# A two-block transformer kernel: expert queries and projection tiles as three one-pass products, and a table of zeros stored earlier

## The reference

```python
h = modulate(rmsnorm_2(x, norm1_g), shift1, scale1)
proj = h @ w_in                          # 1024 -> 512 + 128 + 128 + 3 * 512
q, k, v, cb, cc, cu = jnp.split(proj, SPLITS, axis=-1)
q = rope(rmsnorm_2(q, q_norm_g)); k = rope(rmsnorm_2(k, k_norm_g))
attn = sliding_window_attention(q, k, v, sinks)        # window 128, 8 heads, 2 kv heads
conv = cb * short_conv(cc * cu, conv_w)
merged = concatenate([rmsnorm_2(attn, attn_out_g), rmsnorm_2(conv, conv_out_g)])
x = x + gate1 * (merged @ w_out)
h2 = modulate(rmsnorm_2(x, norm2_g), shift2, scale2)
x = x + gate2 * peer(h2, wq, subkeys, u_tab, v_tab)
```

## Time and profile before

| | |
|---|---|
| time, median of 3 runs | 2406.66 us (2406.08 to 2408.51) |
| profiled execution, its own time | 2408.77 us |
| its span | 2407.0 us |
| mean granted TensorE clock | 0.992 |

### The profile page before, as it was taken

How to read it: one execution, slowest core, us unless ns; L and a number is a source line. 1 busy time by engine, 2 the same in 40 slices (tenths; PEclk the granted TensorE clock), 3 DMA queues, 4 the chain that set the end, 5 groups by cost and what they waited for, 6 DMA issues and landing times.

```text
span 2407.0 us, 33349 instructions
## 1 busy us (share of the span) xinstructions
PE 2371.8 (99%) x11315; PEld 1444.0 (60%) x11315; DVE 1445.1 (60%) x2831; ACT 874.4 (36%) x1385; POOL 1065.4 (44%) x739
## 2 busy tenths in 40 slices
PE   8999899999999999999999999999999999999999
PEld 6888677668888865445544444444444566666665
DVE  4512376366968456436948893222222498999998
ACT  3222134232232342223135555454545433333332
POOL 0001121010000020001888888888888165578886
PEclk9999799999999999999999999999999999999999
DMA  7240100165746313941446666666667799999997
GB/s 208 71 73 1 49 18 32 69 190 146 233 133 195 81 53 102 382 144 54 88 71 155 148 154 151 154 151 151 155 147 164 260 408 371 370 362 371 366 374 285
DMA packets 437699, 426.47 MB, mean 177 GB/s; under 512 B 104808, under 2 KB 359912, under 8 KB 437488
## 3 DMA queue, kind: packets, MB, share of 16 engines
q1 hardware_dynamic: 353456, 332.85, 43.3%
q0 software_dynamic: 84160, 92.58, 15.6%
HBM read 364.28 MB, written 61.05 MB: 177 GB/s over the span
## 4 chain that ended last, share of the span: by engine, by line
PE 86%; DVE 2%; ACT 1%; issue 0%; POOL 0%; DVEq 0%; ACTq 0%; POOLq 0%
PE psum L1473 9%; PE psum L1474 9%; PE psum L1475 9%; PE psum L1496 7%; PE psum L1498 7%; PE psum L1497 7%; PE psum L1248 6%; PE psum L1205 5%; PE psum L1207 5%; PE psum L1206 5%; PE psum L1454 4%; PE psum L968 1%; PE psum L1194 1%; PE psum L1092 1%; PE psum L988 1%; PE psum L1048 1%
## 5 line engine op out<-in xcount | busy, mean ns | idle before, releaser
L785 POOL DMA_INDIRECT dense_gates<-arena x384 | 607.2, 1581 | 151.6 <-issue 116.7
L1473 PE MATMUL psum<-arena 128*128 128x512 bf16 x1024 | 389.4, 380 | 0.0
L1475 PE MATMUL psum<-arena 128*128 128x512 bf16 x1024 | 387.2, 378 | 0.0
L1474 PE MATMUL psum<-arena 128*128 128x512 bf16 x1024 | 386.6, 378 | 0.0
L2542 DVE TENSOR_TENSOR arena<-arena,psum 128x1024 bf16<-128x1024 f32 x124 | 151.5, 1222 | 352.2 <-ACT psum L1854 351.6
L1497 PE MATMUL psum<-arena,low 128*128 128x384 bf16 x1024 | 333.8, 326 | 0.0
L1498 PE MATMUL psum<-arena,low 128*128 128x384 bf16 x1024 | 333.8, 326 | 0.0
L1496 PE MATMUL psum<-arena,low 128*128 128x384 bf16 x1024 | 333.8, 326 | 0.0
L1870 ACT ACTIVATE low<-low 128x1024 bf16<-128x1024 f32 x128 | 135.3, 1057 | 297.7 <-PE psum L1498 278.4
L813 POOL DMA_INDIRECT arena<-gelu_spill,arena x128 | 184.0, 1438 | 87.0 <-DMA gelu_spill<-cst 43.3
L805 POOL DMA_INDIRECT arena<-in_v,arena x128 | 177.4, 1386 | 86.7 <-DVE arena L2589 59.2
(11 more groups left out here) (378 smaller groups left out, 3910.5 us busy)
## 6 DMA issues: line engine op xcount, KB each, us to landing
arena<-in_uT SPq DMA_DIRECT2D x128, 512.0 KB, 4.6
low<-in_v SPq DMA_DIRECT2D x128, 512.0 KB, 5.5
gelu_spill<-cst SPq DMA_DIRECT2D x128, 256.0 KB, 3.4
arena<-in_ada_w POOLq DMA_DIRECT2D x12, 2048.0 KB, 9.3
dense_gates<-arena SPq DMA_DIRECT2D x4, 6144.0 KB, 40.0
arena<-gelu_spill SPq DMA_DIRECT2D x128, 192.0 KB, 5.7
arena<-dense_gates SPq DMA_DIRECT2D x128, 192.0 KB, 6.9
low<-in_w_in SPq DMA_DIRECT2D x20, 1024.0 KB, 7.3
```

The source lines that it names most:

```text
L785: pool.indirect_dma_start(gate_cells, bass.IndirectOffsetOnAxis(ap=cell_of[:, n:n + 1], axis=0), gate_of[:, n:n + 1], None, compute_op=ALU ...
L1473: mm(psum[:, bank, :], hi[:, c, :], h2hi[:, c, :], start=c == 0, stop=False)
L1474: mm(psum[:, bank, :], hi[:, c, :], h2lo[:, c, :], start=False, stop=False)
L1475: last = mm(psum[:, bank, :], lo[:, c, :], h2hi[:, c, :], start=False, stop=c == DC - 1)
```

## The change

Fifteen tiles of the second block's projection (n = 0, 1: the query tiles f = 2, 3; n = 2: the key tile; n = 3 to 14: the convolution) and the queries u = 2 to 15 are made from halves: ScalarE copies the weight tile into one of four float32r tiles (`s_high`, `q_high`), VectorE subtracts and writes the low half over the tile in its slot (`second_low`, `query_low`), and TensorE makes high x high and low x high over all chunks and then high x low. The modulated input is split too, chunk by chunk: on ScalarE the high halves; on GpSimd the low halves of chunks 0 to 4 (`LOWS_POOL`) in the second block and of all eight for the queries, on VectorE those of chunks 5 to 7 in the second block. The low half for the queries is written over `u2`, so GpSimd waits for the last half query too. `take_half` and `half_scores` move within ScalarE's order, `AHEAD` goes from 20 to 15 and `slots_of(1)` into `choose`. `zeros` lies in `turned`; GpSimd sets it before the first attention, and SP stores it in sixteen DMAs, two or three behind each load of gate sums; VectorE waits for them before its first use of `turned`.

```diff
-PARTS, AHEAD = 8, 20
+PARTS, AHEAD = 8, 15
+LOWS_POOL = 5
+ZEROS = 16
@@ SP, first attention, for h in range(FH)
                 sp.dma_start(cb[:, h % 2, :], sums[h:h + 1, :].to_broadcast([P, T])).then_inc(S[f"sums_in{h % 2}"], 16)
+                if h == 0:
+                    sp.wait_ge(S["pool_step"], 10)
+                else:
+                    for q in range((h - 1) * ZEROS // (FH - 1), h * ZEROS // (FH - 1)):
+                        sp.dma_start(io["dense"][q * PK // ZEROS:(q + 1) * PK // ZEROS, :, 0:DEN].rearrange("i j t -> j i t"),
+                                     zeros.unsqueeze(1).to_broadcast([P, PK // ZEROS, DEN])).then_inc(S["zeroed"], 16)
@@ SP, second block
-            sp.wait_ge(S["pool_step"], 10)
-            for q in range(4):
-                sp.dma_start(io["dense"][q * 32:(q + 1) * 32, :, 0:DEN].rearrange("i j t -> j i t"),
-                             zeros.unsqueeze(1).to_broadcast([P, 32, DEN])).then_inc(S["zeroed"], 16)
@@ GpSimd
+            for c in range(LOWS_POOL):
+                pool.wait_ge(*second_part("l2_sq", c + 1))
+                pool.tensor_tensor(s_operand_low[c], u2[:, c, :], s_operand_high[c], ALU.subtract).then_inc(S["g_nm"], 1)
...
+            for c in range(DC):
+                pool.wait_ge(S["h2_split"], c + 1)
+                pool.wait_ge(*operand_part("ffn_sil", c + 1))
+                pool.wait_ge(*operand_part("ffn_ps", c + 1))
+                pool.tensor_tensor(u2_low[c], u2[:, c, :], u2_high[c], ALU.subtract).then_inc(S["sq_sum"], 1)
@@ TensorE
+            def second_product(n, bank, sig, between=None):
+                pe.wait_ge(*second_part("x_nrm", n + 1))
+                wh, wl, out = s_high[n % 4], second_cols(n, slot_halves), psum[:, bank, :]
+                for c in range(DC):
+                    if n == 0:
+                        pe.wait_ge(*second_part("l2_sq", c + 1))
+                    if between and c == 4:
+                        between()
+                    mm(out, wh[:, c, :], s_operand_high[c], start=c == 0, stop=False)
+                    mm(out, wl[:, c, :], s_operand_high[c], start=False, stop=False)
+                for c in range(DC):
+                    if n == 0:
+                        pe.wait_ge(*(second_part("g_nm", c + 1) if c < LOWS_POOL else second_part("l2_done", c - LOWS_POOL + 1)))
+                    last = mm(out, wh[:, c, :], s_operand_low[c], start=False, stop=c == DC - 1)
...
@@ TensorE, expert queries
-                for c in range(DC):
-                    last = mm(psum[:, u % 2, :], w[:, c, cols], u2[:, c, :], start=c == 0, stop=c == DC - 1)
+                for c in range(DC):
+                    mm(out, wh[:, c, :], u2_high[c], start=c == 0, stop=False)
+                    mm(out, wl[:, c, :], u2_high[c], start=False, stop=False)
                     if u == 2 and c == 1:
                         for k in range(2):
                             half_scores(k, 1)
+                for c in range(DC):
+                    last = mm(out, wh[:, c, :], u2_low[c], start=False, stop=c == DC - 1)
@@ ScalarE, second block
-            shift(0, 0)
+            shift(0, 0, first_highs)
+            second_operand_high(0, 4)
...
+                if f == 0:
+                    second_operand_high(4, DC)
+                    second_high(2)
...
+                for n in {0: (7,), 1: (8,), 2: (9, 10), 3: (11,), 4: (12, 13), 5: (14,)}.get(s, ()):
+                    second_high(n)
@@ VectorE, second block
             modulated(0, col_n1, DC)
+            for n in range(2):
+                second_low(n)
+            for c in range(LOWS_POOL, DC):
+                dve.wait_ge(*second_part("l2_sq", c + 1))
+                dve.tensor_tensor(s_operand_low[c], u2[:, c, :], s_operand_high[c], ALU.subtract).then_inc(S["l2_done"], 1)
             dve.wait_ge(S["std_ready"], 5)
             settle(dve.reciprocal(r2[:, 1, :], r2[:, 1, :]))
...
                     last_norm(2 * j + 1)
+                if j == 0:
+                    second_low(2)
+            second_low(3)
+            second_low(4)
             rotate(4)
+            second_low(5)
...
+                for n in {0: (6,), 1: (7,), 2: (8,), 3: (9, 10), 4: (11,), 5: (12, 13), 6: (14,)}.get(s, ()):
+                    second_low(n)
@@ VectorE, choice of experts
+            lows = {(0, 2): 3, (0, 6): 4, (1, 4): 5, (1, 7): 6, (2, 2): 7, (2, 4): 8, (2, 7): 9}
+            for piece, (t0, t1) in enumerate(((0, 1), (1, 2), (2, SC))):
                 for part in range(PARTS):
+                    if (piece, part) in lows:
+                        query_low(lows[piece, part])
                     choose(0, part, t0, t1)
                 slots_of(0, t0, t1)
             for k in range(PARTS, AHEAD):
+                if k < PARTS + 6:
+                    query_low(k + 2)
                 choose(*divmod(k, PARTS))
```

More of the change, by code:

```diff
@@ L133, in program @@
         arena_floats = 53200 - n_const - 64
+        with nc.sbuf_tensor("split_low", [P, CUT], F32R) as split_low:
+            pass
         low = ctx.enter_context(nc.sbuf_tensor("low", [P, CUT], F32))
@@ L136, in program, with halves_room @@
             pass
+        def halves_room(name, at, n):
+            start = (at - CUT) // 8 * 8
+            lead = at - CUT - start
+            with ExitStack() as before:
+                if start:
+                    before.enter_context(nc.sbuf_tensor(f"before_{name}", [P, start], F32))
+                return before.enter_context(nc.sbuf_tensor(name, [P, lead + n], F32R))[:, lead:lead + n]
+        NORM_AT, LAST_AT, RING_AT = CUT, 28035, 35619
+        halves_norm = halves_room("halves_norm", NORM_AT, (DC + 2) * SEC)
+        halves_last = halves_room("halves_last", LAST_AT, 2 * SEC)
+        halves_ring = halves_room("halves_ring", RING_AT, 8665)
+        SECOND_AT = 36872
+        halves_second = halves_room("halves_second", SECOND_AT, 2 * DC * SEC + 4 * DC * P)
         arena = ctx.enter_context(nc.sbuf_tensor("arena", [P, arena_floats - CUT], F32))
@@ L710, in _ @@
             pool.memset(rstd[:, :, T:TP], 0.0).then_inc(S["pool_step"], 1)
+            pool.wait_ge(S["table_in"], 32)
+            step(pool.memset(zeros, 0.0))
             pool.wait_ge(S["gate_tok"], NT)
@@ L1416, in half_query @@
                               start=c == 0, stop=c == DC - 1)
-                if c == DC - 1:
+                    if half and u:
+                        last.then_inc(S["ffn_ps"], 1)
+                if c == DC - 1 and not (half and u):
                     last.then_inc(S["wq_done"], 1)
@@ L1780, in _ @@
                     qk_root(4)
+                    second_high(3)
+            for n in (4, 5, 6):
+                second_high(n)
             def take_c(j):
@@ L1835, in _, with query_high, take_half @@
             std2(5, 6, 0, eps)
+            def query_high(u):
+                if u in (2, 4, 8, 12):
+                    act.wait_ge(*fill_done(F_WQ + u // 4))
+                if u >= 6:
+                    act.wait_ge(S["wq_done"], u - 2)
+                f_(q_high[u % 4], q_raw(u), ACT.Copy).then_inc(S["fw_hi"], 1)
+            SH = SEC // 2
+            def take_half(u, half):
+                if half and u:
+                    act.wait_ge(*operand_part("ffn_ps", DC))
+                else:
+                    act.wait_ge(S["wq_done"], 2 * half + u + 1)
+                f_(qf[:, u, half * SH:(half + 1) * SH], psum[:, 6 * half + u, 0:SH], ACT.Copy).then_inc(S["wq_taken"], 1)
+            query_high(2)
             shift(1, 3 * DC)
@@ L1913, in _ @@
                 u_high(n + 3, n + 3, first=n == 0)
-                h = n // PARTS + 3
-                if n == 0:
-                    weigh_slots(2)
-                elif n % PARTS == PARTS - 1 and h < PH:
+                h, part = divmod(n + 1 + AHEAD, PARTS)
+                if part == 4 and h < PH:
                     weigh_slots(h)
```

149 lines of the change are left out of this document (107 added, 42 removed).

## The result

The changed kernel takes 2392.0 us in the median of five runs (2386.91 to 2393.64), the kernel before beside it 2406.66 (2405.11 to 2408.91): a ratio of 0.9932 with an interval from 0.9921 to 0.9944. It is faster, by 14.7 us or 0.7%, clear of the noise though a small gain, and my forecast of 2378.5 (2368 to 2390) was too low. The profiled execution took 2392.0 us with a span of 2390.2; the span of before was 2407.0, so the spans differ by 16.8 us where my sum had 27.9.

What follows compares the result with a forecast made beforehand. TensorE, busy for 99% of the span, was taken to bound the kernel. -8.7 us up to the output projection and -19.2 us in the queries gave -27.9, so 2378.5 us from 2406.66, range 2368 to 2390.

Steps and rivals of the forecast that it cites:

- Up to the window: Second block before the first window scores: VectorE's serial chain makes this part 7.0 us later, despite four replaced products.
- all eleven gains count: 15.7 us: Window attention, tiles n = 4 to 14: each product's 1.43 us gain counts in full, 15.7 us together.
- D: From output projection to first half query: forecast change 0.
- A: From the start until VectorE ends the second block's modulation: forecast change 0.
- E: From first half query to the experts' first gelu: fourteen shorter query products, less 0.8 us, forecast -19.2 us.
- 0.8 us is lost (ends: 0 and 3): Query product u = 2: waiting for GpSimd's low halves loses 0.8 us of its gain, between 0 and 3.
- it costs nothing, but narrowly: Gates' scatter before the down products: later start stays hidden, with 6 us of slack left of 30.
- The second rival: Gates' scatter: first scatter later still; 14 us more would cost 8 us, giving 2386.5; chance 0.14.
- The zeros: First attention: sixteen zero stores between row loads, at most 4.6 us each, stay hidden; no gain.
- stretches at the slow clock after 926: Second block after 926: TensorE's slow clock stays, losing about 10 us instead of 2.65, giving 2386; chance 0.08.
- two records per matmul: Replaced products: float32r runs in two records of 0.43 us like float32, +3.43 x 29, giving 2506; chance 0.01.
- the first rival: Whole change: all new work is hidden, -41.5 us, giving 2365; chance of landing under 2371: 0.12.

Runs made afterwards that it cites:

- the last run: Tile 3's subtraction earlier and all eight low halves on GpSimd, without the last 16 of 384 indirect DMAs, against the kernel with both edits: 2378.63 us.
- the aligned kernel: Tile 3's subtraction earlier, all eight low halves on GpSimd, and one-pass operands starting at multiples of 128 bytes, against the kernel before: 2378.56 us, ratio 0.9872.

## Why the prediction was wrong, point by point

**Up to the window: right.** The forecast was +7.0 us, measured are 57.19 - 50.23 = 7.0. Its steps are all in VectorE's timeline:

```profile
884.86 3.09 DVE L2503 TENSOR_TENSOR halves_second<-arena,halves_second 128x512 fp32r<-128x512 f32 x3 [3.65 <-ACT halves_second L1879]
887.88 3.34 DVE L2505 RECIPROCAL arena<-arena 128x512 f32<-128x512 f32 x1
...
891.38 3.35 DVE L2537 RECIPROCAL arena<-arena 128x512 f32<-128x512 f32 x1
...
925.78 2.36 DVE L2495 TENSOR_TENSOR split_low<-low,halves_second 128x1024 fp32r<-128x1024 f32 x2
```

The normalizations start at 891.38 for 890.3 + 0.7 forecast, tile 3's subtraction at 925.78 and TensorE goes on at 927.05 (926.5 + 0.7). The three subtractions beside GpSimd's five took 3.09 us where 0.69 each make 2.1: contention cost 1.0 us, the value I took and not the 5 at the other end. It was that little because VectorE had waited 3.65 us, while most of GpSimd's five (880.24 to 886.81) passed. With the wait the clock fell as in the earlier trace rows; the windows say 0.64, 0.50, 0.51 and back at 1.00 by 932 (columns: us, TensorE busy, granted clock, DMA share, GB/s):

```profile
924.00:928.00 4.00, 0.95 (x2) 0.64 1.09 360
928.00:930.00 2.00, 2.00 (x6) 0.50 0.43 138
930.00:932.00 2.00, 2.00 (x5) 0.51 0.00 0
932.00:936.00 4.00, 4.00 (x17) 1.00 0.01 4
```

**The window: the step that failed is "all eleven gains count: 15.7 us".** It was 11.9. The gain of one product was mis-sized: at mean steps of 0.2345 and 0.2387 us instead of the earlier trace rows's 0.2267, the eleven take (5 x 0.0078 + 6 x 0.0120) x 24 = 2.7 us more. And in one round VectorE was late after all, 1.23 us at 968.29, with 0.41 at tile 6 for 0.50 before:

```profile
968.29 1.09 PE L1447 MATMUL psum<-cst,arena 128*128 128x128 f32 x8 [1.23 <-DVE arena L2592]
```

Together 3.8 us. I had carried a duration from one stretch to another as a constant of the instruction. Of the 2.7, 1.2 to 1.4 went when the start addresses were aligned (three runs); the rest has no cause that a run shows.

**The output projection: a loss that no step had.** D is 1.7 us longer, though neither the projection nor the 1.98 us wait ahead of it changed. The granted clock did. Before, that wait is at 1046.49 and TensorE goes on at 1048.47; in the changed kernel it is at 1042.28 and TensorE goes on at 1044.26 (before, then changed, the window behind the wait; the granted clock is the third number from the end):

```profile
1048.00:1052.00 4.00, 3.53 (x9) 1.65 (x10) 4.00 (x5) 0.00 (x0) 0.00 (x0) 1.00 0.02 4
```

```profile
1044.00:1048.00 4.00, 3.74 (x5) 1.65 (x6) 4.00 (x5) 0.00 (x0) 0.00 (x0) 0.57 0.00 0
```

Over the kernels D is 61.59 nine times and 63.28 or 63.29 four times, with the same 1.98 us of idleness before it each time, and without regard to what was edited. So 1.7 us of my miss are where the clock happened to fall in the profiled run. The same holds for the +0.7 in A: A is 878.25 with the queries alone, which has the same stores there.

**The queries: the same step length, and u = 2.** E is -15.3 for -19.2. Thirteen rounds went from 7.76 us (6.87 and 0.89 for the scores) to 6.45, 1.31 each where I had 1.43: 1.5 us of the 3.9. The rest is the start: of my "0.8 us is lost (ends: 0 and 3)" the far end came, about 3.2 us. TensorE waits twice for GpSimd's low halves:

```profile
1132.23 0.50 PE L1555 MATMUL psum<-halves_norm,halves_ring 128*128 128x512 f32 x1 [0.74 <-POOL halves_norm L861]
1133.47 0.80 PE L1555 MATMUL psum<-halves_norm,halves_ring 128*128 128x512 f32 x1 [0.74 <-POOL halves_norm L861]
```

And the clock fell behind them, which my sum did not have (before, then changed):

```profile
1134.00:1136.00 2.00, 2.00 (x6) 0.88 (x5) 1.92 (x13) 0.00 (x0) 1.54 (x1) 1.00 0.00 0
```

```profile
1134.00:1136.00 2.00, 2.00 (x6) 1.55 (x5) 1.97 (x4) 1.55 (x2) 0.00 (x0) 0.50 0.00 0
```

Until 1136.7 the steps were 0.43 us, which cost TensorE about 1.6 us. Unlike the fall before the output projection this one is regular: all eleven kernels with queries from halves have it behind this wait, and the two with float32 queries don't. No run took the wait away.

**The gates: "it costs nothing, but narrowly" failed, by 1.1 us.** The second rival (gates late, chance 0.14) had the mechanism right; its 14 us did not come. The last scatter ends at 1867.91 + 1.55 = 1869.5, forecast 1854.2. Of these 15.3 us, 6.2 are the parts before the half queries, which I had too short. The first scatter stands 1139.02 - 1107.54 = 31.5 us behind the first half query, for 24.4 before: 7.1 us, where I had 4.5. And the row itself takes 1867.91 - 1139.02 = 728.9 us for 1856.81 - 1134.46 = 722.4; the page gives its 384 instructions 613.7 us for 607.2:

```profile
L868 POOL DMA_INDIRECT dense_gates<-arena x384 | 613.7, 1598 | 122.3 <-issue 116.7
```

Nor was the landing "by about 1857", 2.8 us after the last scatter: SP's load of the gates starts 5.7 us after its end. Since the down products, too, were due 10 us later than forecast, only 1.1 us shows. That SP's queue holds the gates up (theory 2 of the last run) is excluded by its timeline, too: it issues nothing from 1870.9 until the scatters have landed.

```profile
1870.34 0.52 SPq L729 DMA_DIRECT2D arena<-gelu_spill  x1
1875.20 1.75 SPq L721 DMA_DIRECT2D arena<-dense_gates  x4
```

**The zeros: right.** A is 878.25 with the queries alone, stores in the first attention included, and 878.13 before. The sixteen took 10.3 us from issue to landing (median, two or three being under way at once) where I had 4.6 for one, and no load that anybody waited for stood behind them. The rivals of stretches at the slow clock after 926 and of two records per matmul did not occur; the first rival, everything hidden, failed at the steps named above.

**Sum of the misses:** A 0.7, C 3.8, D 1.7, E 3.9, F 1.1 = 11.2 us, and 27.9 - 16.8 = 11.1 is what was missing.

**The range** was too narrow by its own terms. The bounds that I named for the unknown costs, taken together, reach 2378.5 + 4 + 7.35 + 2.2 + 8 = 2400 and not 2390.

## What to carry to other kernels

When a product becomes cheaper, look at what it used to cover: here VectorE's serial chain and then a row of indirect DMAs took over, and two small edits (a subtraction put before the normalization that it stood behind, three subtractions given to the idle engine) were worth about half as much as the change: from column B on the change gained 17.5 us, both edits another 9.9, and 8.4 with aligned operands. The lowest median is that of the aligned kernel, 2378.56 us, ratio 0.9872 to before, for 0.9932; part of it is column A, 4.0 us shorter in its profile. Edits at a wait don't add singly: one alone moves the wait. Whether the clock falls behind a short one did not repeat: of five kernels with a wait of 1.83 to 1.88 us at the last rotation, three lost the clock there and two kept it. And compare short experiments by stretches between fixed events: a kernel's first 878 us differed by up to 5.8 us with equal instructions. The clock goes with it: in the four kernels with A below 875 us the granted clock from 292 to 300 was 1.00, in the others 0.50.

## What the hardware showed unexpectedly

- A one-pass float32r matmul of 128x512 took 0.2267 us from step to step in the feed-forward part, and mostly 0.23 to 0.24 us elsewhere at the same granted clock of 1.00. The step can change within a product. With the operands' start at a multiple of 32 bytes the 0.240 became 0.232 to 0.234, and the last eight matmuls of each window product 0.2267; at 128 bytes no more was gained.
- An idle time of 1.98 us before the output projection was followed by a granted clock of 0.57 (window 1044 to 1048) in the changed kernel and of 1.00 (1048 to 1052) in the one before. The same wait costs 1.7 us or nothing.
- A tiny VectorE instruction can lose a whole microsecond beside GpSimd. A CAST of 128x16 took 0.17 us before, and 1.13 and 1.24 us beside the last of GpSimd's eight subtractions; that is 2.0 of the 7.1 us by which the first scatter is late (before, then changed, then GpSimd's):

```profile
1129.69 0.17 DVE L2497 CAST arena<-arena 128x16 f32<-128x16 uint32 x1
```

```profile
1131.08 1.13 DVE L2677 CAST arena<-arena 128x16 f32<-128x16 uint32 x1
1132.13 0.16 DVE L2678 CAST arena<-arena 128x16 f32<-128x16 uint32 x1
1132.20 1.24 DVE L2680 CAST arena<-arena 128x16 f32<-128x16 uint32 x1
```

```profile
1130.89 2.53 POOL L861 TENSOR_TENSOR halves_norm<-arena,halves_last 128x512 fp32r<-128x512 f32 x2
```

  The Trainium skill (SBUF — State Buffer, "SBUF: two separate sides") has GpSimd and a VectorE instruction that has two SBUF inputs, or runs in a two-port mode, lock each other out for whole instructions. These rows agree: the short instruction waits for the rest of a GpSimd one of 1.28 us, and the long CASTs end at 1132.21 and 1133.44, GpSimd's two at about 1132.2 and 1133.42. Whether a CAST here runs in such a mode no row says. MAX8 and FIND_INDEX8 of 128x256 lost nothing beside GpSimd: 0.43 and 0.41 us there, 0.43 and 0.42 before. In the second block the lock cost only 1.0 us, since little of GpSimd's work lay beside VectorE's there (880.24 to 886.81 against 884.86 to 887.95).
- With aligned operands F was 659.6 us, though its first down product waited 1.8 us for the gates: so the rest of that stretch ran about 2 us faster, and the row of scatters took that back. Which operand did it was not tried.
